# First expert pair's operand from marks and x1 tiles on PE instead of a gather; slot 4's weights behind the last tile's store

## The reference

```python
x1 = layernorm(ALPHA * x + mix)                      # ALPHA = 2 ** 0.25
g_sel = argmax(x1 @ w_group + b_group)               # 1 of 4 groups
top_i = top_k(e_logits[g_sel] + e_bias, 2)           # 2 of the 8 experts of that group
y     = sum over the 2 experts of gate * (silu(gu[:, :256]) * gu[:, 256:]) @ w_down[e],  gu = x1 @ w_gate_up[e]
out   = layernorm(ALPHA * x1 + y)
```

## Time and profile before

| | us |
|---|---|
| median of 3 runs (lowest, highest) | 596.57 (596.06, 598.97) |
| profiled execution, own time | 594.66 |
| its span | 593.0 |
| PE busy | 515.9 |
| DVE busy | 372.8 |
| ACT busy | 190.9 |
| POOL busy | 134.4 |

### The profile page before, as it was taken

One profiled execution on the slowest core, in us unless ns is written; L12 is line 12 of the kernel. 1 busy time (PEld: TensorE's weight loads), 2 busy tenths in 40 slices (PEclk: granted clock), 3 DMA queues, 4 the chain that ended last, 5 costly groups with the idle time before them and its releaser, 6 DMA issues.

```text
span 593.0 us, 8961 instructions
## 1 busy us (share of the span) xinstructions
PE 515.9 (87%) x3296; PEld 279.5 (47%) x3296; DVE 372.8 (63%) x722; ACT 190.9 (32%) x356; POOL 134.4 (23%) x156
## 2 busy tenths in 40 slices
PE   6999999999989879999999898888887667767762
PEld 5887788874355533455457743332332222222220
DVE  0752049898954577643178665678886567756686
ACT  0100375204244642140232122445444334432340
POOL 1001045510026740000000202333323231221231
PEclk9999999999999999999999999999999999999997
DMA  8950008580607832002978599999999999999951
GB/s 302 385 187 6 1 0 318 194 312 1 253 34 293 345 142 61 2 35 102 425 279 328 198 422 414 402 398 418 415 416 410 420 416 419 415 414 419 405 203 46
DMA packets 34298, 157.95 MB, mean 266 GB/s; under 512 B 12712, under 2 KB 12712, under 8 KB 20304
## 3 DMA queue, kind: packets, MB, share of 16 engines
q1 hardware_dynamic: 20880, 127.46, 53.7%
q0 software_dynamic: 10752, 29.59, 13.2%
q10 hardware_dynamic: 2624, 0.34, 0.4%
HBM read 160.12 MB, written 21.23 MB: 306 GB/s over the span
## 4 chain that ended last, share of the span: by engine, by line
PE 58%; DMA 24%; DVE 7%; ACT 6%; issue 3%; SPq 1%; POOL 0%; DVEq 0%; POOLq 0%; ACTq 0%
DMA arena_o<-in_w_gu 19%; PE ps L496 17%; PE ps L968 8%; PE ps L752 8%; PE ps L991 4%; PE ps L597 3%; PE ps L659 2%; PE ps L643 2%; PE ps L917 2%; PE ps L680 2%; DMA first_rows<-arena_s,known 1%; PE ps L815 1%; DMA known<-slot_table 1%; PE ps L563 1%; DMA slot_table<-arena_s 1%
## 5 line engine op out<-in xcount | busy, mean ns | idle before, releaser
L968 PE MATMUL ps<-arena_w,arena_s 128*64 128x512 f32 x368 | 107.6, 595 | 25.2 <-DMA arena_o<-in_w_gu 11.7
L496 PE MATMUL ps<-arena_w 128*128 128x260 f32 x416 | 95.4, 390 | 5.4 <-DMA arena_w<-in_xT 4.8
L496 PEld LDWEIGHTS ps<-arena_w 128*128 128x128 f32 x416 | 79.9, 194 | 20.4 <-DMA arena_w<-in_xT 5.6
L968 PEld LDWEIGHTS ps<-arena_w,arena_s 128*64 128x64 f32 x368 | 32.8, 137 | 96.9 <-issue 66.8
L991 PE MATMUL ps<-arena_w,cs 128*64 128x512 f32 x184 | 56.5, 618 | 20.8 <-ACT cs L1267 20.8
L752 PE MATMUL ps<-arena_o,arena_s 128*128 128x512 f32 x128 | 58.2, 600 | 0.8 <-DVE arena_s L1612 0.8
L968 PE MATMUL ps<-arena_o,arena_s 128*64 128x512 f32 x112 | 50.2, 595 | 0.0
L1484 DVE STREAM_TRANSPOSE arena_s<-arena_w 128x1024 f32<-128x1024 f32 x36 | 42.1, 1217 | 8.1 <-PE ps L597 8.1
L2161 POOL DMA_INDIRECT first_rows<-arena_s,known x15 | 18.0, 1199 | 113.2 <-ACT arena_s L1274 104.3
L1921 DVE TENSOR_TENSOR arena_s<-arena_s,ps 128x256 f32<-128x256 f32 x16 | 6.7, 421 | 56.0 <-ACT arena_s L1263 56.0
L991 PEld LDWEIGHTS ps<-arena_w,cs 128*64 128x64 f32 x184 | 16.2, 140 | 51.1 <-issue 30.4
(11 more groups left out here) (349 smaller groups left out, 894.9 us busy)
## 6 DMA issues: line engine op xcount, KB each, us to landing
arena_w<-in_w_gu SPq DMA_DIRECT2D x46, 1024.0 KB
arena_w<-in_w_dn SPq DMA_DIRECT2D x23, 1024.0 KB
...
```

What stands on the lines that cost most here:

```text
L496: last = mm(ps[rows, b + n, 0:HALF], lhs(k), rhs(k)[:, n * HALF:(n + 1) * HALF], start=(k == 0), stop=(k == ks - 1))
L968: last = mm(ps[64 * e:64 * e + 64, 2 + q, :], xgT[:, k, CAP * e:CAP * (e + 1)], gu_w[2 * slots + e][:, k, :], start=(k == 0), stop=(k == K ...
```

## The change

- **Operand of pair 0.** `first_known` and `mark_first` on DVE make, for each token, a row of 128 marks: 1 at the slot that the token has in pair 0. `first_tokens(m)` on PE multiplies x1 tile m (8 blocks of 128 columns) with these marks and sums over the five tiles, which gives the transposed operand in the PSUM banks where `turn_tokens(0)` put it. Tiles 0 to 2 come while DVE chooses the last tile's experts, tile 3 of the order after its rank, the last one after the slot numbers. `logits` of the last tile move to bank 5, since banks 0 and 1 are now taken.
- **Gathers.** Pair 0's rows are still gathered, for the residual. POOL's order is 1, 0, then a wait for the operand, then 2, 3. The bound of the row numbers is held in a register.
- **SP.** Slot 4's weights follow the last x1 store without a wait. The waits for all stores and for `xt_ps` (pair 0's operand) stand before the `lng` tables.
- **Order after it.** PE runs `experts(0)` before the loop of `slot_numbers` and `slot_facts`. DVE copies pair 0's operand out before the gates, and does `hidden(0)` and the copies of pair 1 between the third and fourth payload row. ACT copies pair 0 before its two Exp and does `hidden(0)` before it waits for `routed`.

```diff
@@ -236,6 +236,8 @@
         facts = part(arena_s, S_RT, NV7, NPAIR)
         table = part(arena_s, S_TAB, NQ, NF, QUAD)
         first_at = part(arena_s, S_TAB + NF * NPAIR, NPAIR).bitcast(I32)
+        first_mark = part(arena_s, S_E, TT, P)
+        in_first = part(arena_s, S_E + TT * P, 3, 2, TT)
         turn_i = part(arena_s, S_RT + 260, 2, TT).bitcast(I32)
         turn_f, far = part(arena_s, S_RT + 270, 2, TT), part(arena_s, S_RT + 280, 2, TT)
         me, oh1, oh2, rt_t = (part(arena_s, S_RT + 360 + 160 * n, TT, NE) for n in range(4))
@@ -348,7 +350,7 @@
 
         def logit_bank(m):
 
-            return ps[:, 6, 0:NL] if m < 2 else ps[:, m % 2, 0:NL]
+            return ps[:, 6 if m < 2 else 5 if m == TT - 1 else m % 2, 0:NL]
 
         def rotation(eng, n):
 
@@ -441,11 +443,11 @@
                 gate_up(3, slice(3, 4), half)
             down(3, slice(3, 4))
             store_x1(4)
-            landed(sp, x1_stored, TT)
-            landed(sp, gathered[0])
             for half in range(2):
                 gate_up(4, slice(4, 5), half)
             down(4, slice(4, 5))
+            landed(sp, x1_stored, TT)
+            sp.wait_ge(xt_ps, 1)
             sp.dma_start(lng, lns[0:2].partition_broadcast(P)).then_inc(ln1_landed, 16)
             sp.dma_start(lng2, lns[2:4].partition_broadcast(P)).then_inc(ln1_landed, 16)
             def refill(q, e, used):
@@ -924,18 +926,30 @@
             turn_x1(4)
             keep_warm(5, 4)
             logits(4)
-            pe.wait_ge(slots_ready, 1)
+            def first_tokens(m):
+
+                t, n = ORDER[m], ROWS[ORDER[m]]
+                pe.wait_ge(ln_norm, m + 1)
+                for k in range(KD):
+                    last = mm(ps[:, k // 4, (k % 4) * P:(k % 4 + 1) * P], x1[0:n, t, k * P:(k + 1) * P], first_mark[0:n, m, :],
+                              start=(m == 0 and k % 4 == 0), stop=(m == TT - 1), skip_group_check=True)
+                return last
+
+            pe.wait_ge(lg_out, TT)
             ranks(TT - 1, range(TT - 1))
             totals(range(TT - 1))
-            slot_numbers(range(TT - 1))
-            keep_warm(9, 4)
+            for m in range(3):
+                first_tokens(m)
+            keep_warm(3, 4)
             pe.wait_ge(route_dve, 2)
             ranks(TT - 1, [TT - 1])
             totals([TT - 1]).then_inc(rank_ps, 1)
-            keep_warm(4, 4)
+            first_tokens(3)
+            pe.wait_ge(slots_ready, 1)
+            slot_numbers(range(TT - 1))
             pe.wait_ge(slots_ready, 2)
             slot_numbers([TT - 1]).then_inc(slots_ps, 1)
-            keep_warm(28, 4)
+            first_tokens(4).then_inc(xt_ps, 1)
             def slot_facts():
                 for kt in range(2 * TT):
                     for e in range(2):
@@ -992,9 +1006,7 @@
                                       dn_w[2 * slots + e][:, f, h * 512:(h + 1) * 512], start=(f == 0), stop=(f == 1))
                 last.then_inc(dn_ps, 1)
 
-            turn_tokens(None, 0)
-
-            first = products(None, 0)
+            experts(None, 0, *products(None, 0))
             pe.wait_ge(routed, 1)
             n_rounds = pe.value_load(rounds[0:1, 0:1], min_val=1, max_val=MAXR)
             past = pe.value_load(rounds[0:1, 1:2], min_val=0, max_val=(MAXR - 1) * NPAIR)
@@ -1004,7 +1016,6 @@
                 slot_numbers(range(TT), ps[:, 7, NV7 * NPAIR:NV7 * NPAIR + NE])
                 slot_facts().then_inc(facts_ps, 1)
 
-            experts(None, 0, *first)
             for n in range(1, HEAD):
                 experts(None, n, *products(None, n))
             with pe.Fori(0, n_rounds * 2 - 1) as it:
@@ -1252,11 +1263,11 @@
                               bias=vec[:, V_LB + k:V_LB + k + 1], scale=vec[:, V_LG + k:V_LG + k + 1])
                 last.then_inc(xt_act, 1)
 
+            tokens_out(None, 0)
             act.wait_ge(route_dve, 3)
             fn(rt_t[:, :, 0:NG], rt_t[:, :, 0:NG], ACT.Exp).then_inc(route_act, 1)
             act.wait_ge(route_dve, 4)
             fn(rs[:, 6:8, :], rs[:, 6:8, :], ACT.Exp).then_inc(route_act, 1)
-            tokens_out(None, 0)
 
             def hidden(it, n, last_pair=False):
                 act.wait_ge(gu_ps, nth(it, n, add=1))
@@ -1289,10 +1300,12 @@
                 src = slot_table[k * P:(k + 1) * P, :] if isinstance(k, int) else slot_table[bass.ds(k * P, P), :]
                 act.dma_start(known[:, n // QUAD % 2, :, :].rearrange("p f n -> p (f n)"), src[:, QUAD:NF * QUAD]).then_inc(known_landed, 16)
 
+            hidden(None, 0)
             act.wait_ge(routed, 1)
             n_rounds = act.value_load(rounds[0:1, 0:1], min_val=1, max_val=MAXR)
             for n in range(HEAD):
-                hidden(None, n)
+                if n > 0:
+                    hidden(None, n)
                 if n == 0:
                     act.wait_ge(slots_ready, n_rounds + 2)
                 own_out(None, n)
@@ -1708,6 +1721,20 @@
                 link(tt(prod[:, :, a:b, :], both[:, :, a:b, :],
                         ps[:, 2, a * NE:b * NE].rearrange("p (t e) -> p t e", t=b - a).unsqueeze(1).broadcast_to([P, 2, b - a, NE]), ALU.mult))
                 link(V.tensor_reduce(rs[:, 14:16, a:b], prod[:, :, a:b, :], AX_X, ALU.add))
+
+            def first_known(a, b):
+
+                step(tt(in_first[:, 0, :, a:b], both[:, 0, a:b, 0::NPAIR].rearrange("p t e -> p e t"),
+                        both[:, 1, a:b, 0::NPAIR].rearrange("p t e -> p e t"), ALU.add))
+
+            def mark_first(a, b):
+
+                link(tt(in_first[:, 1, :, a:b], prod[:, 0, a:b, 0::NPAIR].rearrange("p t e -> p e t"),
+                        prod[:, 1, a:b, 0::NPAIR].rearrange("p t e -> p e t"), ALU.add))
+                link(stt(in_first[:, 2, :, a:b], in_first[:, 1, :, a:b], -1.0, in_first[:, 0, :, a:b], ALU.add, ALU.add))
+                return tt(first_mark[:, a:b, :].rearrange("p t (e c) -> p t e c", e=2),
+                          count_sb[:, :].unsqueeze(1).unsqueeze(1).broadcast_to([P, b - a, 2, CAP]),
+                          in_first[:, 2, :, a:b].rearrange("p e t -> p t e").unsqueeze(3).broadcast_to([P, b - a, 2, CAP]), ALU.is_equal)
 
             def mark_slots(a, b):
                 return tt(slot_mark.rearrange("p (n t) c -> p n t c", n=2)[:, :, a:b, :],
@@ -1792,18 +1819,23 @@
             mixed(15)
             dve.wait_ge(o_out, 16)
             moments1(4)
+            dve.wait_ge(dec_mixed, 1)
+            first_known(0, 4)
             dve.wait_ge(rank_ps, 1)
             x1T_out(4)
             scale1(4)
             rank_of(0, 4)
-            mark_slots(0, 4).then_inc(slots_ready, 1)
+            step(mark_first(0, 4))
             logits_out(4)
             choose_group(4, TT)
             choose_expert(4, TT).then_inc(route_dve, 1)
             dve.wait_ge(route_dve, 2)
             number_parts(4, TT)
+            first_known(4, TT)
+            mark_slots(0, 4).then_inc(slots_ready, 1)
             dve.wait_ge(rank_ps, 2)
             rank_of(4, TT)
+            step(mark_first(4, TT))
             mark_slots(4, TT).then_inc(slots_ready, 1)
             rank = rs[:, 14:16, :].rearrange("p a b -> p (a b)")
 
@@ -1816,6 +1848,19 @@
             link(tt(work[:, 2, :], work[:, 2, :], work[:, 3, :], ALU.add))
             stt(first_at[:, :], work[:, 1, :], -1.0, work[:, 2, :], ALU.add, ALU.add).then_inc(first_ready, 1)
 
+            def tokens_out(it, n):
+                dve.wait_ge(xt_ps, nth(it, n, add=1))
+                if n > 0:
+                    dve.wait_ge(gu_ps, nth(it, n))
+                for k in range(KD // 2):
+                    last = ts(xgT[:, k, :], ps[:, k // 4, (k % 4) * P:(k % 4 + 1) * P], vec[:, V_LG + k:V_LG + k + 1],
+                              vec[:, V_LB + k:V_LB + k + 1], ALU.mult, ALU.add)
+                last.then_inc(xt_sb, 1)
+            def hidden(it, n):
+                dve.wait_ge(silu_done, nth(it, n, add=1))
+                tt(hx, sg, ps[:, 2 + n % 2, DE:2 * DE], ALU.mult).then_inc(h_ready, 1)
+
+            tokens_out(None, 0)
             link(V.tensor_reduce(rs[:, 3, :], L[:, :, 0:NG], AX_X, ALU.max))
             tt(rt_t[:, :, 0:NG], L[:, :, 0:NG], per(rs[:, 3, :], NG), ALU.subtract).then_inc(route_dve, 1)
 
...
@@ -1871,6 +1907,9 @@
                 last = tt(payload[:, :, :, c, :], held, flags[:, c, :].unsqueeze(2).unsqueeze(3).broadcast_to([P, 2 * TT, 2, NPAIR]), ALU.mult)
                 if c < NV7 - 1:
                     step(last)
+                if c == 2:
+                    hidden(None, 0)
+                    tokens_out(None, 1)
             last.then_inc(facts_ready, 1)
             link(V.tensor_reduce(rs[:, 13, 0:1], ps[:, 7, 0:NE], AX_X, ALU.max))
             link(ts(rs[:, 13, 1:2], rs[:, 13, 0:1], float(CAP - 1), None, ALU.add))
...
@@ -1976,11 +2011,10 @@
                     finish(it, n - 2)
                 own_part(it, n)
 
-            hidden(None, 0)
-            tokens_out(None, 1)
             n_rounds = slot_tables()
```

(10 more changed lines are left out.)

18 lines of the change are left out of this document (3 added, 15 removed).

## The result

The changed kernel takes 602.54 us (median of 9 runs, 600.76 to 604.41), the kernel before 598.75 in the same comparison (595.96 to 600.22). The ratio is 1.0084, 95% interval [1.0061, 1.0107]: slower by some 5 us (the two medians alone are 3.8 us apart). The prediction said 600.5, slower, with a range of 595.5 to 605.

A forecast was written before the change was run, and what follows sets the result against it. The prediction took the weight stream to set the end, its refill waiting for PE half through pair 3. The operand's 0.7 us gain and the later table left PE 3.9 us later: 596.57 + 3.9 = 600.5 us, range 595.5 to 605.

The forecast's parts named there:

- The end follows PE's half of pair 3: SP's weight refill at 382.48 waits for PE half through pair 3; the kernel's end is that time plus a constant.
- the dry queue: Expected sign of being right: SP's weight queue empty for several microseconds before a refill near 386.
- the three signs of being wrong: Pair 5's refill issued by 382.5, a queue never empty between 375 and 386, or pair 1's SiLU released by PE.
- Slot 4's early place gives nothing: SP's three transfers at 322.6 instead of 335.16 take 7.6 us from the crowded stretch; no gain unless PE is earlier.
- Rival 1: Weight stream after 338: if it always had work, three units less bring the end 7.6 us forward, to 589; chance 0.09.
- Operand on PE: Pair 0: operand matmuls replace the gather's wait and transposes; last tile's rank 4.6 us later, `products(0)` only 0.7 us earlier.
- rival 2: First 24 operand matmuls: the clock does not drop, everything 1.6 us earlier, +2.3, 598.9; chance 0.16.
- Rival 4: First 24 operand matmuls: the clock stays low through all of them, +7.9, 604.5; chance 0.08.
- Two register loads, 0.8 us: PE between `experts(0)` and the slot facts: the loads take 0.8 us, bounds 0 and 1.6.
- ACT kept by the table: Table 5.4 us later, less 0.9 slack: ACT free at 363.35, `experts(1)` at 365.6 against 361.73, PE 3.9 us later.
- Rival 3: Table store of 3.4 us or less: ACT free before PE needs it, only PE's own path left, +1.3, 597.9; chance 0.15.
- Sum: Whole kernel: half of pair 3 at 386.4, the refill and everything behind it 3.9 us later, median 600.5.

The follow-up runs named there:

- g_slot4_late: a_gates_early with slot 4's weight transfers put back behind SP's waits for the stores and pair 0's operand; ratio 1.0005 to the kernel before, median 598.0 us.
- a_slot4_late: The changed kernel with slot 4's weight transfers put back behind SP's waits for the stores and pair 0's operand; ratio 1.0052 to the kernel before.
- a_loads_behind: The changed kernel with ACT's wait for the table store and its two loads moved behind `hidden(1)`; ratio 1.0028 to the kernel before.
- a_gates_early: The changed kernel with DVE's gate arithmetic in its waits, ACT's Exp ahead of its copies, slot facts ahead of `experts(0)`; ratio 0.9954 to before, median 595.5 us.
- b_slot4_early: The kernel before with only slot 4's three weight transfers moved directly behind the last x1 store; ratio 1.0091 to before, median 602.6 us.
- a_small_tile_first: The changed kernel with the 8-row tile among the first 24 operand matmuls and a full tile behind the ranks; ratio 1.0070 to the kernel before.
- b_delay_pair1: The kernel before with 24 warming matmuls (5.6 us) on PE ahead of the products of pair 1; ratio 1.0075 to the kernel before.
- b_delay_pair7: The kernel before with 24 warming matmuls (5.6 us) on PE ahead of the products of pair 7; ratio 1.0029 to the kernel before.
- g_warm_gap: a_gates_early with seven warming matmuls added on PE behind the last operand group; ratio 0.9975 to the kernel before.

## Why the prediction was right, and where its sizes were not

**The end follows PE's half of pair 3: right, with a condition.** Both delays and the dry queue show it, and none of the three signs of being wrong came. It holds while the queue drains first; g_slot4_late is the case where it doesn't. The prediction read 0.44 MB from 382 to 384 as a queue that ran dry about as the refill was issued. It ran at nearly full rate until then (0.77 MB from 380.4 to 382.4) and dipped behind it: the reading is about a microsecond off, and by these rows before had about that microsecond of room until bytes would have counted.

**Slot 4's early place gives nothing: right in after, and only there.** a_slot4_late isn't told from after. What the prediction overlooked is its price beside a gather: alone it costs 5.4 us in before. Rival 1 (the filled hole pays, 589) is out by 13 us.

**Operand on PE: right in sign, mis-sized by the clock.** Predicted was `products(0)` 0.7 us earlier, with 6.7 of the first 24 matmuls at half clock. In after these ran at full clock (5.60 us for 24, the 0.233 each of the earlier trace rows), the rank of the last tile came at 331.29, 12.8 us behind the first mark where 14.8 had been forecast, and `products(0)` could have been 2.4 us earlier, as in a_slot4_late and a_loads_behind (1.9 in a_gates_early). The half clock came later instead: 1.2 us in the last group, 2.9 in `products(0)`. So rival 2 was right on the place and wrong on the sum: the drop was not absent, it came later. Rival 4, half clock through all 24, is out by the 1.00 of 325.20 to 330.80. The Trainium skill, "TensorE: Matmul & The Clock Gate", section "Why this matters for your kernels", puts a drop down to an idle gap. That fits the drops at 369 (PE busy 1.30 of 4.00 before it) and in b_slot4_early (idle 4.17), and it does not fit those at 324 in before and in a_small_tile_first, with PE busy throughout, nor the one at 334.6 in after, where the two microseconds of 331.4 to 333.4 were full, nor the one at 312 in a_loads_behind, with PE busy 3.00 of 3.00 us from 308 to 311.

**Two register loads, 0.8 us: wrong, the lower bound holds.** `experts(0)` ends at 355.28 and the facts' first matmul is at 355.41, 0.13 later, with `routed` there since 353.48 + 0.15 = 353.63, 1.65 us ahead of that end. Had the two loads begun only at that end, the gap would be 0.8 to 1.6 by the prediction's own bounds. The Trainium skill, "TensorE: Matmul & The Clock Gate", section "Architectural detail: the array is 16× 32×32, not 1× 128×128", gives TensorE a queue of 64 instructions; it does not speak of register loads there, and the gap is what such a queue would allow. `routed` itself was forecast for 349.8 and came at 353.63 - 1.53 = 352.1; the difference of 2.3 is mostly that of `products(0)`, behind which `hidden(0)` stands.

**ACT kept by the table: right, and one consequence missed.** From the end of the facts to ACT free of its two issues the prediction had 353.1 to 363.35, 10.25 us; measured 356.41 to 366.78, 10.37. From ACT to `experts(1)` 2.2 was forecast, 2.1 measured. `experts(0)` to `experts(1)` came to 17.30 and 16.80 for a forecast of 18.0, the loads' 0.8 being most of the difference. Missed was that PE, having waited 3.42 us (2.8 to 2.9 in a_slot4_late and a_small_tile_first), goes on at half clock: 1.4 to 1.7 us more in the following step. a_loads_behind takes out both. Rival 3 (PE's own path ends last) is excluded by the SiLU's row at 366.83.

**Sum.** Forecast +3.9; the profile reads 72.65 - 65.48 = +7.2 and a_slot4_late, with its drop ahead of the marks, +2.4. The ratio says +5.0 [3.7, 6.4]. (The 600.5 adds 3.9 to the 596.57 of the first runs; on the 598.75 of the comparison it would be 602.7.) That the forecast lies so near is partly luck. The half clock that it had put into the first 24 matmuls (1.6 us) was not there; 1.2 and 2.9 us of half clock at pair 0 and 1.5 in pair 1, which it did not have, were. What I can show of the +5.0: 3.3 us are ACT's place (the ratios of after and a_loads_behind, 1.0084 and 1.0028; with both intervals between 1.3 and 5.3), the facts 1.1, the operand -1.9 to -2.4. The other 2.5 to 3 us are not shown; the clock at pair 0 is a weak candidate for them, since before's own instructions lost 1.7 us there too in b_delay_pair1 and b_delay_pair7. Which executions lose it, and where, stays open: two attempts to steer it (a_small_tile_first, g_warm_gap) failed. a_loads_behind, at a ratio 1.7 us above before, looks 1.2 us faster by its marks. The half clock ahead of its first mark would account for that: its refill goes out at 385.36, where b_delay_pair7 has 385.41 and before 382.48. Marks that begin behind a drop leave it out, so a sum of steps is to be compared only with one whose drops lie within the same marks.
